# A recurrence's gate projections: the second and fourth weight sums of each strip formed by VectorE instead of GpSimd

## The chip, the cores and the metric

One core of one Trainium2 chip runs the whole program. The metric is device microseconds of one execution, the median of several runs. The engines named here are TensorE (PE in the profile, its weight loads apart as PEld), VectorE (DVE), ScalarE (ACT), GpSimd (POOL) and the DMA queue issued by SyncE (SPq).

## What is computed

Two transformer blocks of two layers each work on 256 latent and 256 context tokens, batch 1, in float32. The change lies in the first layer of the first block, an HGRN2 mixer with 16 heads of width 128:

```
q, i_in, f_fw, f_bw, z = jnp.split(h @ w_in, 5, axis=-1)     # h: 512 x 1024, w_in: 1024 x 10240
log_f = jnp.logaddexp(jnp.log(lbd), jnp.log1p(-lbd) + jax.nn.log_sigmoid(gf))
k = (1.0 - lbd) * jax.nn.sigmoid(-gf)
# per direction, a chunkwise scan  S_t = diag(f_t) S_{t-1} + k_t v_t^T,  o_t = S_t^T q_t
o = _rmsnorm(o, o_gain);  y = (o * silu(z)) @ w_out
```

Everything after it (latent attention, and the second block with its branches and convolutional feed-forward) is untouched.

## The kernel before

The engines' programs are written out by hand, each in its own order, and meet through semaphores. The mixer works on its 16 heads in 8 pairs. While the *core* of pair i-1 (the scan) runs, the *projections* of pair i run between its steps. This interleaving is a "round"; rounds 1 to 7 hold a core and projections, pair 0's projections stand ahead of them, and pair 7's core behind them is interleaved with the output projection.

A round's projections are five strips of w_in, 1024 x 256 each, loaded into five slots of `ring_mem`. Strips 0 to 3 (one forget gate, the readout gate z, the query, the other forget gate) are computed by a Strassen-Winograd scheme of seven products where eight would be plain: `hg_seven_tensor`, with `hg_parts` naming the quarters a11, a12, a21, a22 of a strip. Each product is 4 contraction steps of 128x128 weights against 256 tokens, all on line 805 (8 matmul instructions in the trace). The sums of tokens are made once, ahead of the rounds (`T_hg`, held in `xT`). The sums of weights are made for each strip:

- `S1_hg` = a21 + a22 (line 2301) and a21 := a11 - a21 (line 2302, raises `s3_ready`), by VectorE in `hg_sums_vector` at the end of the gathering of the strip before.
- a11 := S1_hg - a11 (line 2911, raises `s2_ready`) and a12 := a12 - a11 (line 2914, raises `s4_ready`), by GpSimd. These are the two that the change touches. They overwrite the strip in place, so the first must wait until product *one* has read a11, the second until product *two* has read a12: it waits for ScalarE's copies of those products out of PSUM (`one_kept`, line 1829; `two_kept`, line 1842).

TensorE's order in strip j of a round is, at step 2j: products one (a11), seven (a21), two (a12), seven's second half (a22); then a scan step's scores (line 911; two of them at step 0) and at some steps a conditioning product (line 544). At step 2j+1: product five (S1_hg); then **six** (a11, after `two_kept` and `s2_ready`); then five's second half (a12, after `five_kept` and `s4_ready`), which frees the strip; then the next scan step's scores.

VectorE's order is: for each scan step (`hg_scores_vector`) a key product (line 2256), a query product (line 2258, after TensorE's scores of the step), two predicated copies out of PSUM (line 2261), a product of totals (line 2263). After scan steps 1, 3, 5 and 7 comes the gathering of strip 0, 1, 2 and 3 (`hg_gather_vector`): part two plus one (line 2307), plus six (line 2309, after `six_full`, raises `u_ready`), then lines 2313, 2315 and 2318, then the next strip's first two sums. After scan step 4 VectorE multiplies the readout gate (line 2324), after step 6 the query (line 2328), each behind a ScalarE sigmoid (line 1860).

GpSimd has, besides those two sums of each strip, two copies at a round's end (`move_pool`, lines 2895 and 2899).

`nth(i, j)` is the count that a semaphore raised once a strip has reached by strip j of round i.

Of the kernel before, what the change touches and what calls it, by code (L numbers as in the profile page):

```python
# [42 lines left out]
def raised(n):  # L43


    return n + 1
# [112 lines left out]
def build(nc, w, const, out):  # L159

    F32, I32 = mybir.dt.float32, mybir.dt.int32
    ALU, ACT, AX = mybir.AluOpType, mybir.ActivationFunctionType, mybir.AxisListType.X
    V, S, PE = nc.vector, nc.scalar, nc.tensor
    ctx = ExitStack()
    with ctx:
# [3 lines left out]
        def sem(name):  # L169
            return ctx.enter_context(nc.semaphore(name))  # L170
# [4 lines left out]
        def view(ap, *dims, at=0):  # L175

            return bass.AP(ap.tensor, ap.offset + at, [list(ap.ap[0])] + [list(d) for d in dims])
# [59 lines left out]
        S1_hg = kT_flat[:, 0:512].rearrange("p (k n) -> p k n", k=4)  # L237
# [73 lines left out]
        if at.at > b_tables:  # L311
# [54 lines left out]
        one_kept, two_kept, five_kept, seven_kept = sem("one_kept"), sem("two_kept"), sem("five_kept"), sem("seven_kept")  # L366
        s3_ready, s2_ready, s4_ready, t_ready, u_ready, whole_ready = (
            sem("s3_ready"), sem("s2_ready"), sem("s4_ready"), sem("t_ready"), sem("u_ready"), sem("whole_ready"))
# [228 lines left out]
        def strip(name, j, k):  # L597
            return ring.slot(name, j).rearrange("p (k n) -> p k n", k=k)
# [186 lines left out]
        def nth(i, j):  # L785

            return i * 4 + (j - 3)

        def hg_parts(j):


            wj = strip("hg_in", j, 8)
            return wj[:, 0:4, 0:128], wj[:, 4:8, 0:128], wj[:, 0:4, 128:256], wj[:, 4:8, 128:256]
# [769 lines left out]
        def up_halves(l):  # L1563
            (_, a0, a1), (_, b0, b1) = halves(l)
            c0 = CTX * l
            return slice(c0 + a0, c0 + a1), slice(c0 + b0, c0 + b1), a1 - a0
# [253 lines left out]
        def hg_part(j, at, n):  # L1820
            return hg_whole[j][:, at:at + n]
# [474 lines left out]
        def hg_sums_vector(dve, st, i, j):  # L2296


            a11, _, a21, a22 = hg_parts(j)
            ring.wait_loaded(dve, "hg_in", j, i)  # L2300
            st.link(V.tensor_tensor(S1_hg, a21, a22, ALU.add))
            V.tensor_tensor(a21, a11, a21, ALU.subtract).then_inc(s3_ready, 1)

        def hg_gather_vector(dve, st, i, j):
            dve.wait_ge(one_kept, nth(i, j))
            dve.wait_ge(two_kept, nth(i, j))
            V.tensor_tensor(hg_part(j, 0, 256), hg_part(j, 0, 256), P1_hg, ALU.add)
            dve.wait_ge(six_full, nth(i, j))
            V.tensor_tensor(P1_hg, P1_hg, ps[:, 0, 256:512], ALU.add).then_inc(u_ready, 1)
            dve.wait_ge(u_ready, nth(i, j))  # L2310
            dve.wait_ge(seven_kept, nth(i, j))
            dve.wait_ge(five_kept, nth(i, j))
            st.link(V.tensor_tensor(hg_part(j, 256, 512).rearrange("p (s t) -> p s t", s=2), view(P1_hg, (0, 2), (1, 256)),
                                    P57_hg.rearrange("p (s t) -> p s t", s=2), ALU.add))
            st.mark(V.tensor_tensor(hg_part(j, 768, 256), hg_part(j, 512, 256), P57_hg[:, 0:256], ALU.add))
            dve.wait_ge(strips_used, ring.stages["hg_in"]["first"] + i * 5 + (j + 1))
            st.settle()
            V.tensor_tensor(hg_part(j, 256, 512), hg_part(j, 256, 512), ps[:, 1, :], ALU.add).then_inc(whole_ready, 1)
            if j < 3:
                hg_sums_vector(dve, st, i, j + 1)  # L2320
# [569 lines left out]
        def move_pool(pool, i):  # L2890

            if not (isinstance(i, int) and i == 0):
                pool.wait_ge(st_ready, i)
            wait_apart(pool, act_freed, i * 6 + 4)
            nc.gpsimd.tensor_copy(Tw, f_st.rearrange("p d c -> p (d c)"))
            if not (isinstance(i, int) and i == 0):
                pool.wait_ge(o_full, raised(i * 2))
            wait_apart(pool, act_freed, i * 6 + 6)
            nc.gpsimd.tensor_copy(v_w, v_st).then_inc(moved, 1)

        @block.gpsimd
        def _(pool):
            pool.dma_start(ident, const["ident"]).then_inc(tab_loaded, 16)
            pool.dma_start(masks_i, const["masks"]).then_inc(msk_loaded, 16)
            move_pool(pool, 0)
            with pool.Fori(1, PAIRS) as i:
                for j in range(4):
                    a11, a12, _, _ = hg_parts(j)
                    pool.wait_ge(s3_ready, nth(i, j))
                    pool.wait_ge(one_kept, nth(i, j))  # L2910
                    nc.gpsimd.tensor_tensor(a11, S1_hg, a11, ALU.subtract).then_inc(s2_ready, 1)
                    pool.wait_ge(two_kept, nth(i, j))
                    pool.wait_ge(s2_ready, nth(i, j))
                    nc.gpsimd.tensor_tensor(a12, a12, a11, ALU.subtract).then_inc(s4_ready, 1)
                move_pool(pool, i)
            pool.wait_ge(o_ready, raised(2 * PAIRS))
            pool.dma_start(ctx2_in, w["ctx_2"][0].rearrange("(g p) d -> p g d", p=128)).then_inc(ctx2_loaded, 16)
            nc.gpsimd.memset(poolw, 0.0).then_inc(pool_step, 1)
            for dst, name in ((cosb, "cosb"), (sinb, "sinb"), (rotb, "rotb"), (cosm, "cosm"), (sinm, "sinm"), (rotm, "rotm"),
                              (amask, "amask"), (poolm, "poolm"), (dftm, "dftm"), (dftc, "dftc")):  # L2920
                pool.dma_start(dst, const[name]).then_inc(tab_loaded, 16)
            pool.wait_ge(pool_step, 1)
            for l in range(2):
                for g in range(4):
                    e = g % 2 * 64
                    pool.dma_start(poolw[e:e + 64, l, g // 2, e:e + 64], w["pool_w_2"][l, g]).then_inc(tab_loaded, 16)

            steps = Steps(pool, pool_step)
            steps.n = 1
            G = nc.gpsimd  # L2930
            for l in range(2):
                a, b, hw = up_halves(l)
                h_rest, h_top = hT[:, 4:8, b], hT[:, 0:4, b]
                pool.wait_ge(h_ready, h_end[f"mix{l}_b"])
                G.tensor_tensor(T_mg[:, 0, :, 0:hw], h_rest, h_top, ALU.subtract).then_inc(mg_turned, 1)
                G.tensor_tensor(T_mg[:, 3, :, 0:hw], h_top, hT[:, 0:4, a], ALU.subtract).then_inc(mg_turned, 1)
                pool.wait_ge(mg_turned, 4 * l + 2)
                G.tensor_tensor(T_mg[:, 1, :, 0:hw], h_rest, T_mg[:, 3, :, 0:hw], ALU.subtract).then_inc(mg_turned, 1)
                pool.wait_ge(mg_turned, 4 * l + 3)
                G.tensor_tensor(T_mg[:, 2, :, 0:hw], hT[:, 4:8, a], T_mg[:, 1, :, 0:hw], ALU.subtract).then_inc(mg_turned, 1)  # L2940
                for s in range(MS):
                    a11, a12, _, _ = mg_parts(l, s)
                    sums = S_mg[s % 2]
                    pool.wait_ge(mg_first_sums, MS * l + s + 1)
                    steps.link(G.tensor_tensor(sums[:, 1], sums[:, 0], a11, ALU.subtract))
                    G.tensor_tensor(sums[:, 3], a12, sums[:, 1], ALU.subtract).then_inc(mg_sums, 1)

                pool.wait_ge(y_ready, raised(8 * l + 8))
                for f in range(FT):
                    t, j = f // 4, (f + 2) % 4  # L2950
                    ring.wait_loaded(pool, f"up{l}", j, t)
                    sums = S_up[:, f % 2]
                    a11, a12, a21, a22 = up_parts(l, f)
                    if f >= 2:
                        pool.wait_ge(first_sums_ready, (FT - 2) * l + f - 1)
                    else:
                        steps.mark(G.tensor_tensor(sums[:, 0], a21, a22, ALU.add))
                        G.tensor_tensor(sums[:, 2], a11, a21, ALU.subtract)
                        steps.settle()
                    steps.link(G.tensor_tensor(sums[:, 1], sums[:, 0], a11, ALU.subtract))  # L2960
                    G.tensor_tensor(sums[:, 3], a12, sums[:, 1], ALU.subtract).then_inc(sums_ready, 1)
# [95 lines left out]
```

## Time and profile before

| | |
|---|---|
| median of 3 runs | 2458.71 us (2458.56 to 2460.6) |
| the profiled execution | 2456.85 us, of which the profile's span is 2455.0 us |
| PE busy | 2382.2 us, 97% of the span |
| DVE busy | 1323.9 us, 54% |
| ACT busy | 597.3 us, 24% |
| POOL busy | 365.4 us, 15% |
| granted TensorE clock over the span | 0.994 of full speed |

The rounds lie between about 116 and 745 us. Shares over the whole span mix many stages. A round is read from the timeline, which lists each engine's instructions in order of their start, in microseconds from the span's start.

### The profile page before, as it was taken

What the parts mean: (1) busy time and instruction counts of PE and PEld (TensorE: products, weight loads), DVE (VectorE), ACT (ScalarE), POOL (GpSimd) and SP (SyncE); (2) the same over time, 40 slices, a digit from 0 to 9 for tenths busy, and PEclk for the clock granted to TensorE, in tenths of its full rate; (3) what the DMA queues carried; (4) which work ended last, traced back from release to release, by engine and by line L of the source; (5) the groups of instructions that cost most, each with busy time, mean ns of one, the idle gap of its engine ahead of it and who ended that gap; (6) DMA issues with size and microseconds to landing.
All of it is one profiled execution on the core that took longest, in us unless ns stands there. A gap on an engine that the chain in (4) does not pass through costs nothing.

```text
span 2455.0 us, 35576 instructions
## 1 busy us (share of the span) xinstructions
PE 2382.2 (97%) x14660; PEld 1930.0 (79%) x14660; DVE 1323.9 (54%) x2240; ACT 597.3 (24%) x1203; POOL 365.4 (15%) x250
## 2 busy tenths in 40 slices
PE   7999999999998999999999999999999999999999
PEld 3588888888875688668877778788884787999988
DVE  3186787787787233441263332366668335437951
ACT  3133333333222032342241000221110023113211
POOL 0012223222210100000101111022210000322310
PEclk9999999999998999999999999999999999999999
DMA  9433133223250525204311322233348551555662
GB/s 369 171 125 120 68 120 120 94 94 127 96 170 20 159 69 138 69 1 120 88 34 39 99 86 86 60 91 90 87 115 286 199 137 35 155 155 147 166 174 65
DMA packets 320819, 284.88 MB, mean 116 GB/s; under 512 B 27329, under 2 KB 300361, under 8 KB 320185
## 3 DMA queue, kind: packets, MB, share of 16 engines
q1 hardware_dynamic: 319002, 279.08, 37.2%
q0 software_dynamic: 1216, 3.93, 0.4%
q8 instruction: 89, 1.46, 0.2%
q14 instruction: 33, 0.27, 0.0%
q10 hardware_dynamic: 479, 0.13, 0.0%
HBM read 279.98 MB, written 3.15 MB: 115 GB/s over the span
## 4 chain that ended last, share of the span: by engine, by line
PE 87%; DVE 7%; ACT 2%; DMA 2%; issue 1%; SPq 1%; ACTq 0%; DVEq 0%
PE ps L805 13%; PE ps L1576 12%; PE ps L1489 8%; PE ps L1687 5%; PE ps L865 5%; PE ps L1672 4%; PE ps L1543 3%; PE ps L1522 3%; PE ps L911 2%; PE ps L856 2%; PE ps L998 2%; PE ps L1016 2%; PE ps L1090 2%; DVE arena L2668 2%; PE ps L1314 2%; PE ps L544 2%
## 5 line engine op out<-in xcount | busy, mean ns | idle before, releaser
L805 PE MATMUL ps<-hT,ring_mem 128*128 128x256 f32 x672 | 160.2, 381 | 0.0
L805 PE MATMUL ps<-xT,ring_mem 128*128 128x256 f32 x672 | 158.8, 379 | 0.0
L805 PEld LDWEIGHTS ps<-hT,ring_mem 128*128 128x128 f32 x672 | 126.0, 190 | 20.2 <-issue 3.2
L805 PEld LDWEIGHTS ps<-xT,ring_mem 128*128 128x128 f32 x672 | 127.6, 190 | 17.6 <-issue 0.3
L1576 PE MATMUL ps<-hT,arena 128*128 128x256 f32 (+1 forms) x704 | 132.5, 333 | 6.9 <-ACT hT L565 6.9
L468 DVE RECIPROCAL rstd<-root 128x256 f32<-128x256 f32 (+2 forms) x17 | 28.2, 1659 | 201.5 <-ACT root L441 200.4
L1576 PE MATMUL ps<-arena 128*128 128x256 f32 (+1 forms) x704 | 129.6, 327 | 0.0
L1576 PEld LDWEIGHTS ps<-hT,arena 128*128 128x128 f32 x704 | 112.2, 196 | 16.9 <-issue 7.5
L1576 PE MATMUL ps<-hT,ring_mem 128*128 128x256 f32 (+1 forms) x704 | 123.0, 327 | 0.0
L1672 PE MATMUL ps<-arena,ring_mem 128*128 128x512 f32 (+1 forms) x352 | 116.6, 492 | 2.2 <-DVE arena L2678 2.2
L1687 PE MATMUL ps<-arena,ring_mem 128*128 128x256 f32 (+1 forms) x704 | 118.2, 328 | 0.0
L1576 PEld LDWEIGHTS ps<-arena 128*128 128x128 f32 x704 | 109.7, 191 | 9.1
L1576 PEld LDWEIGHTS ps<-hT,ring_mem 128*128 128x128 f32 x704 | 107.9, 191 | 9.7 <-issue 0.6
L1687 PEld LDWEIGHTS ps<-arena,ring_mem 128*128 128x128 f32 x704 | 105.9, 191 | 11.4 <-issue 2.7
L865 PE MATMUL ps<-ring_mem,hT 128*128 128x256 f32 x512 | 113.0, 379 | 0.0
L865 PEld LDWEIGHTS ps<-ring_mem,hT 128*128 128x128 f32 x512 | 96.1, 190 | 12.4
L2960 POOL TENSOR_TENSOR arena<-arena,ring_mem 128x512 f32<-128x512 f32 x44 | 56.0, 1273 | 332.2 <-DVE arena L2686 332.2
L1672 PEld LDWEIGHTS ps<-arena,ring_mem 128*128 128x128 f32 x352 | 67.4, 193 | 48.1 <-issue 40.3
L2564 DVE TENSOR_TENSOR arena<-root,ps 128x256 f32<-128x256 f32 (+1 forms) x24 | 8.5, 354 | 175.4 <-ACT root L2094 124.1
L1489 PE MATMUL ps<-arena 128*128 128x256 f32 (+1 forms) x576 | 98.2, 327 | 0.0
L2608 DVE SCALAR_TENSOR_TENSOR xT<-ps,mod_b,xT 128x256 f32<-128x256 f32 (+1 forms) x60 | 23.5, 425 | 137.3 <-PE ps L1687 57.0
L1489 PEld LDWEIGHTS ps<-arena 128*128 128x128 f32 x576 | 87.8, 191 | 7.4
(348 smaller groups left out, 4669.9 us busy)
## 6 DMA issues: line engine op xcount, KB each, us to landing
ring_mem<-in_w_up_dram SPq DMA_DIRECT2D x88, 512.0 KB, 5.1
ring_mem<-in_hg_w_in_dram SPq DMA_DIRECT2D x40, 1024.0 KB, 5.0
ring_mem<-in_w_in_dram SPq DMA_DIRECT2D x30, 1024.0 KB, 5.5
ring_mem<-in_w_mod_dram SPq DMA_DIRECT2D x12, 2048.0 KB, 7.8
arena<-in_w_mod_dram SPq DMA_DIRECT2D x24, 1024.0 KB, 5.5
ring_mem<-in_w_down_dram SPq DMA_DIRECT2D x16, 1408.0 KB, 7.2
ring_mem<-in_ada_w_dram SPq DMA_DIRECT2D x8, 2048.0 KB, 7.7
ring_mem<-in_mla_w_in_dram SPq DMA_DIRECT2D x9, 1024.0 KB, 5.4
```

The source lines that it names most:

```text
L544: mm = PE.matmul(bank[c * 32:c * 32 + 32, 0:256], sil_cols[:, cond * 16 + 2 * k:cond * 16 + 2 * k + 32], wm[:, k % 4, c * 256:c * 256 + 25 ...
L805: mm = PE.matmul(dst, left[:, k, :], right[:, k, :], start=k == 0, stop=k == 3)
L856: mm = PE.matmul(bank, wj[:, k, m * 128:m * 128 + 128], hT[:, k, :], start=k == 0, stop=k == 7)
L865: mm = PE.matmul(bank[:, g * 256:g * 256 + 256], hT[:, k, tok:tok + 128], wj[:, k, :], start=k == 0, stop=k == 7)
L911: mm = PE.matmul(ps[c:c + w_, LV[b], (u % 4) * 128 + q0:(u % 4) * 128 + q0 + w_], keys, queries, start=True, stop=True)
L1489: mm = PE.matmul(mg_region(l, s, which, hw), left[:, k, :], right[:, k, 0:hw], start=k == 0, stop=k == 3)
L1522: mm = PE.matmul(ps[:, mg_bank(i) + m, 0:n], wj[:, k, m * 128:m * 128 + 128], brT[:, k, c0:T], start=k == k0, stop=k == k1 - 1)
L1543: mm = PE.matmul(ps[:, (0 if part == "_a" else 4) + j, m * (hi - lo):(m + 1) * (hi - lo)], wj[:, k, m * 128:m * 128 + 128], yT[:, k, c0 + ...
L1576: mm = PE.matmul(up_region(f, which, hw), left[:, k, :], right[:, k, 0:hw], start=k == 0, stop=k == 3)
L1672: mm = PE.matmul(ps[:, j, 0:n], wj[:, k, :], hid[:, k, 0:n], start=k == 0, stop=k == FT - 1)
L1687: mm = PE.matmul(ps[:, (4 if part == "_a" else 0) + j, 0:hi - lo], wj[:, k, :], hid[:, k, lo:hi], start=k == 0, stop=k == FT - 1)
L2960: steps.link(G.tensor_tensor(sums[:, 1], sums[:, 0], a11, ALU.subtract))
```

## The change

GpSimd's loop over the four strips is gone; it keeps its two copies. VectorE makes the two sums at the head of `hg_gather_vector`, ahead of its first addition, behind the same waits on `one_kept` and `two_kept`.

```diff
         def hg_gather_vector(dve, st, i, j):
+            a11, a12, _, _ = hg_parts(j)
             dve.wait_ge(one_kept, nth(i, j))
             dve.wait_ge(two_kept, nth(i, j))
+            V.tensor_tensor(a11, S1_hg, a11, ALU.subtract).then_inc(s2_ready, 1)
+            dve.wait_ge(s2_ready, nth(i, j))
+            V.tensor_tensor(a12, a12, a11, ALU.subtract).then_inc(s4_ready, 1)
             V.tensor_tensor(hg_part(j, 0, 256), hg_part(j, 0, 256), P1_hg, ALU.add)
             dve.wait_ge(six_full, nth(i, j))
...
             with pool.Fori(1, PAIRS) as i:
-                for j in range(4):
-                    a11, a12, _, _ = hg_parts(j)
-                    pool.wait_ge(s3_ready, nth(i, j))
-                    pool.wait_ge(one_kept, nth(i, j))
-                    nc.gpsimd.tensor_tensor(a11, S1_hg, a11, ALU.subtract).then_inc(s2_ready, 1)
-                    pool.wait_ge(two_kept, nth(i, j))
-                    pool.wait_ge(s2_ready, nth(i, j))
-                    nc.gpsimd.tensor_tensor(a12, a12, a11, ALU.subtract).then_inc(s4_ready, 1)
                 move_pool(pool, i)
```

The changed lines shift the numbers: line 2307 of before is 2311 in the changed kernel, 2309 is 2313, and the new sums are lines 2308 and 2310.

VectorE's instructions in the body of the loop over the rounds, around the gathering of strip 0. The first row of both is the last one of scan step 1. Before:

```order
L2263 TENSOR_TENSOR arena<-arena 128x1024 [waits merged]
L62 ISA
L2305 ISA [waits dve_step]
L2307 TENSOR_TENSOR arena<-arena 128x256 [waits two_kept,one_kept]
L2309 TENSOR_TENSOR arena<-arena,ps 128x256 [waits six_full]
L2313 TENSOR_TENSOR arena<-arena 128x512 [waits five_kept,seven_kept,u_ready]
```

And now:

```order
L2263 TENSOR_TENSOR arena<-arena 128x1024 [waits merged]
L62 ISA
L2306 ISA [waits dve_step]
L2308 TENSOR_TENSOR ring_mem<-arena,ring_mem 128x4x128 [waits two_kept,one_kept]
L2310 TENSOR_TENSOR ring_mem<-ring_mem 128x4x128 [waits s2_ready]
L2311 TENSOR_TENSOR arena<-arena 128x256
L2313 TENSOR_TENSOR arena<-arena,ps 128x256 [waits six_full]
L2317 TENSOR_TENSOR arena<-arena 128x512 [waits five_kept,seven_kept,u_ready]
```

Two instructions came in behind scan step 1's last product and ahead of the first addition, at each of the four strips; no register instruction came with them.

GpSimd's instructions in the body of its loop. Before, from the third strip on:

```order
L2911 TENSOR_TENSOR ring_mem<-arena,ring_mem 128x4x128 [waits one_kept,s3_ready]
L2914 TENSOR_TENSOR ring_mem<-ring_mem 128x4x128 [waits s2_ready,two_kept]
L2909 REGISTER_ALU
L2911 TENSOR_TENSOR ring_mem<-arena,ring_mem 128x4x128 [waits one_kept,s3_ready]
L2914 TENSOR_TENSOR ring_mem<-ring_mem 128x4x128 [waits s2_ready,two_kept]
L2911 TENSOR_TENSOR ring_mem<-arena,ring_mem 128x4x128 [waits one_kept,s3_ready]
L2914 TENSOR_TENSOR ring_mem<-ring_mem 128x4x128 [waits s2_ready,two_kept]
L36 ISA [waits st_ready]
L2895 COPY arena<-arena 128x2048 [waits act_freed]
```

And now, the whole body:

```order
L36 ISA [waits st_ready]
L2899 COPY arena<-arena 128x2048 [waits act_freed]
L2901 ISA
L36 REGISTER_ALU [waits o_full]
L2903 COPY arena<-arena 128x1024 [waits act_freed]
```

The eight sums of a round left GpSimd, the copies stayed. TensorE's and ScalarE's orders are the same in both kernels.

## Rows read from the trace of the kernel before

**Rows 1.** The page's chain of work that ended last, shares by engine.
```profile
PE 87%; DVE 7%; ACT 2%; DMA 2%; issue 1%; SPq 1%; ACTq 0%; DVEq 0%
```

**Rows 2.** Busy time by engine in one round: window, length, busy (count), PEclk, DMA.
```profile
383.00:472.00 89.00, 87.34 (x695) 74.12 (x694) 70.96 (x93) 29.13 (x45) 22.22 (x11) 1.00 0.31 105
```

**Rows 3.** Waits of PE in 110 to 790 us: us in total, times, longest.
```profile
PE ps L911 <- ACT K_c L1869: 18.0, 9, 6.1
```

**Rows 4.** Timeline, round 4, strip 0: start, duration, engine, line, operation.
```profile
394.47 2.23 DVE L2258 TENSOR_TENSOR arena<-arena 128x1024 f32<-128x1024 f32 x1
...
397.46 1.70 PEld L805 LDWEIGHTS ps<-xT,ring_mem 128*128 128x128 f32 x8
...
399.20 0.42 DVE L2307 TENSOR_TENSOR arena<-arena 128x256 f32<-128x256 f32 x1 [0.20 <-DVE arena L2263]
...
402.02 0.68 DVE L2301 TENSOR_TENSOR arena<-ring_mem 128x512 f32<-128x512 f32 x1
...
402.74 0.69 DVE L2302 TENSOR_TENSOR ring_mem<-ring_mem 128x512 f32<-128x512 f32 x1
```

**Rows 5.** Timeline, round 4, strip 1.
```profile
413.86 0.42 DVE L2307 TENSOR_TENSOR arena<-arena 128x256 f32<-128x256 f32 x1 [0.19 <-DVE arena L2263]
414.02 1.70 PEld L805 LDWEIGHTS ps<-xT,ring_mem 128*128 128x128 f32 x8
```

**Rows 6.** Timeline, round 4, strip 2.
```profile
425.51 1.72 POOL L2914 TENSOR_TENSOR ring_mem<-ring_mem 128x512 f32<-128x512 f32 x1 [2.11 <-ACT arena L1842]
426.01 2.30 DVE L2256 TENSOR_TENSOR arena<-arena 128x1024 f32<-128x1024 f32 x1
...
426.14 1.15 PE L911 MATMUL ps<-arena,K_c 128*64 128x64 f32 x32
...
428.23 1.21 DVE L2258 TENSOR_TENSOR arena<-arena 128x1024 f32<-128x1024 f32 x1
428.84 1.70 PEld L805 LDWEIGHTS ps<-xT,ring_mem 128*128 128x128 f32 x8
...
431.06 0.43 DVE L2307 TENSOR_TENSOR arena<-arena 128x256 f32<-128x256 f32 x1 [0.19 <-DVE arena L2263]
```

**Rows 7.** Timeline, round 4, strip 3.
```profile
440.78 1.15 PE L911 MATMUL ps<-arena,K_c 128*64 128x64 f32 x32
...
442.75 1.21 DVE L2258 TENSOR_TENSOR arena<-arena 128x1024 f32<-128x1024 f32 x1
443.48 1.70 PEld L805 LDWEIGHTS ps<-xT,ring_mem 128*128 128x128 f32 x8
...
445.32 0.42 DVE L2307 TENSOR_TENSOR arena<-arena 128x256 f32<-128x256 f32 x1
```

**Rows 8.** Timeline, round 7, strip 2 and the conditioning product behind it.
```profile
697.58 1.70 PEld L805 LDWEIGHTS ps<-xT,ring_mem 128*128 128x128 f32 x8
697.64 0.42 DVE L2307 TENSOR_TENSOR arena<-arena 128x256 f32<-128x256 f32 x1
...
703.67 1.93 PE L544 MATMUL ps<-ring_mem,sil_cols 128*32 128x256 f32 x32 [1.17 <-DMA ring_mem<-in_ada_w_dram]
```

**Rows 9.** Timeline, pair 7's core, scan step 1, no GpSimd work beside it.
```profile
755.05 2.22 DVE L2258 TENSOR_TENSOR arena<-arena 128x1024 f32<-128x1024 f32 x1
```

**Rows 10.** Timeline of PE alone, instructions behind three idle gaps elsewhere in the program.
```profile
789.07 1.98 PE L911 MATMUL ps<-arena,K_c 128*64 128x64 f32 x32 [2.65 <-ACT K_c L1869]
...
901.86 2.40 PE L1065 MATMUL ps<-hT,ring_mem 128*128 128x256 f32 x10 [2.61 <-issue]
...
2372.31 4.03 PE L1672 MATMUL ps<-arena,ring_mem 128*128 128x256 f32 x10 [2.16 <-DVE arena L2678]
```

**Rows 11.** Busy time by engine, with PEclk, in stretches behind those gaps.
```profile
788.50:795.20 6.70, 6.13 (x40) 3.85 (x41) 4.53 (x8) 0.51 (x1) 0.00 (x0) 0.50 0.01 2
899.30:906.00 6.70, 4.14 (x28) 3.31 (x32) 0.00 (x0) 5.17 (x16) 0.00 (x0) 1.00 0.54 159
...
2372.30:2375.50 3.20, 3.19 (x8) 2.45 (x9) 1.20 (x3) 0.31 (x1) 0.00 (x0) 0.50 0.02 6
```

## The prediction

> **What bounds the kernel now.** I read the chain of waits first: 87% of it is TensorE, 7% VectorE [rows 1]. GpSimd and VectorE therefore matter only where TensorE waits for them. Next the table of windows, one round at a time: in 89 us TensorE is busy 87.34 and VectorE 70.96, at the full clock [rows 2]. VectorE looks as if it had 18 us to spare in a round. Then the list of waits: through the whole recurrence TensorE's largest wait is 18 us, nine times, for the scan's keys from ScalarE [rows 3], and in none does it wait for GpSimd or for VectorE's gathering. So the two sums cost nothing today. What the changed kernel costs is decided in the timeline, by one comparison made at each strip: when does TensorE want a11, and when does VectorE come to its gathering? The weight load ahead of product six is the first; the start of line 2307 is the second, for the new sums stand exactly in its place. The reader is to see that in every strip VectorE is there about when six starts or later, though its average load is low: strip 0 at 399.20 against 397.46 [rows 4], strip 1 at 413.86 against 414.02 [rows 5], strip 2 at 431.06 against 428.84 [rows 6], strip 3 at 445.32 against 443.48 [rows 7].
>
> **What it removes.** GpSimd's 8 sums of a round. Nothing waited for them, so their time itself gives nothing. But one of them held up VectorE: in strip 2 the key product took 2.30 us, while a GpSimd sum that began 0.50 us before it ran [rows 6], and the query product of the same size took 1.21. Some 1.08 us of VectorE's time comes back there, and as much in strip 3, where the same pattern stands. How much of it counts is limited by TensorE's scores, for which the query product waits: in strip 2 they end at 427.29, so it can start near 427.34 instead of 428.23, a gain of 0.89; in strip 3 they end at 441.93, so 441.98 instead of 442.75, a gain of 0.77 [rows 6, 7]. In strip 0 the query product took 2.23 [rows 4], also beside a long GpSimd sum, but in pair 7's core the same product takes 2.22 with GpSimd idle [rows 9]: its access pattern costs that, and nothing comes back.
>
> **What it adds.** Two subtractions of 128x512 on VectorE at each of 28 strips. Line 2302 has the same form and takes 0.69 us; from line 2301 to its dependent 2302 it is 0.72 from start to start [rows 4]. So a11 is ready 0.69 after VectorE's arrival, and a12 1.41 after. Until TensorE's weight load starts I add 0.10; bounds are 0.04, the gap between 2301's end and 2302's start [rows 4], and 0.3. The stall of product six is then arrival + 0.79 - the load of before:
>
> - strip 0: 399.99 - 397.46 = 2.5 us
> - strip 1: 414.65 - 414.02 = 0.6 us
> - strip 2: 431.06 - 0.89 + 0.79 = 430.96, less 428.84 = 2.1 us
> - strip 3: 445.32 - 0.77 + 0.79 = 445.34, less 443.48 = 1.9 us
>
> Together 7.1 us a round. a12 is never late: its 0.72 us lie beside six, whose load takes 1.70. Nor does line 2307, now 1.41 later, make anything late: the next addition needs six, which is late itself. From line 2318 on VectorE waits for TensorE's last product of the strip and its lag starts afresh. At each strip the stall is therefore new and is not carried as a lag of VectorE's.
>
> Does the stall get lost later? The wait for keys at the head of a round [rows 3] is ScalarE's, which stands behind TensorE's own products of that round, so it moves along. At the round's end VectorE's states are needed by TensorE after a long values projection, and GpSimd's copies, unchanged, hang on those. Nothing there absorbs. SyncE's weight loads are issued on TensorE's release of a slot and move with it. Only round 7 differs. In its strip 2 the conditioning product of before ran late, so VectorE arrives with six (697.64 against 697.58); with the key product unblocked there too, the stall is about 0, and what is left falls into the 1.17 us that TensorE waits for a DMA right after [rows 8]. Round 7 costs 5.0. I take rounds 1 to 6 alike: 6 x 7.1 + 5.0 = 47.6 us.
>
> **The clock.** These are new idle gaps of TensorE, so I looked at what gaps of this size did elsewhere. After an idle gap of 2.65 us the granted clock was 0.50, the 1.2 GHz level, through 788.5 to 795.2; after one of 2.16 us it was 0.50 in 2372.3 to 2375.5; after one of 2.61 us it stayed 1.00, 2.4 GHz [rows 10, 11]. Of 13 new gaps above 2 us (7 in strip 0, 6 in strip 2) I let half end in a fall. A stretch like that of 2372.3, busy 3.19 of 3.20 us at half level, loses half of it, 1.6 us; where part of it lies in the gap, less: I take 1.5. That makes 6.5 x 1.5 = 10 us (bounds 0, and 20 gaps x 1.6 = 32 with strip 3's).
> By the Trainium skill (TensorE: Matmul & The Clock Gate, section HAM oscillation) only idle gaps longer than every one that this change makes let the clock fall in a kernel; by that this term is 0. The gap of 2.16 us in this trace speaks against it.
>
> **The sum.** 47.6 + 10 = 57.6 us on the profiled execution of 2456.85 gives 2514.4; the median of the runs, 2458.71, lies 1.86 above that execution, so I forecast **2516 us**. About 0.2% (5 us) is what a measurement of this kernel can tell from no change.
>
> **Rivals.**
>
> 1. *Stalls as worked out, no fall of the clock.* 2458.71 + 47.6 = 2506. For it: the clock is 1.00 throughout the rounds [rows 2] though they hold waits for keys. Against it: two of the three gaps in rows 10. The skill's rule named above leads here.
> 2. *Every gap of 1.9 us or more lets the clock fall.* 20 x 1.6 = 32 on top of 47.6: 2538. For it: two of three. Against it: the third, and strip 3's gap is shorter than any that is seen to do it.
> 3. *The stalls are partly absorbed.* If what TensorE waits for at a round's head did not move with it, 18 us over nine waits [rows 3], up to 2 each, 14 in seven rounds, could take up the stalls: 2458.71 + 34 to 44, about 2498. Against it: that wait's chain starts at TensorE.
> 4. *The other side: VectorE is in time, and it is not slower.* The mechanism is the hold of GpSimd on VectorE. If each of the 8 sums of a round cost VectorE the 1.08 us of the key product [rows 6], 8.6 us would come back in a round against 4 x 1.41 = 5.6 added, and VectorE would run ahead by 0.8 us a strip. It decides where line 2308 starts 0.8 us before six's load: from there no stall is left, and the time is 2459. Against it: the long query product without GpSimd [rows 9], that strip 0 alone would need 2.5 us, and that in strips 2 and 3 TensorE's scores set the limit.
>
> That the change does not do what it says is excluded by the order of instructions: GpSimd's sums are gone and VectorE's stand ahead of its first addition.
>
> **How the numbers follow.** My forecast, with about half of the gaps falling, 0.50; rival 1, 0.25; rival 2, 0.08; rival 3, 0.13; rival 4, 0.04, of which 0.01 would be faster by over 0.2%. The forecast's own case reaches from 2508 to 2524 (3 to 10 falls, and 0.04 to 0.3 us of hand-over at 27 stalls, which is -2 to +5). The range of 2499 to 2531 takes in rival 1 and most of rival 3, and the near side of rival 2; it leaves out rival 4 and the far ends. Faster 0.01, same 0.03, slower 0.96.
>
> **What would show it.** In the changed profile TensorE's list of waits gets a line, line 805 for VectorE's sum of a11 (line 2308), some 27 times, 45 to 50 us in total, the longest near 2.9. A round gets 96 us or more long against 89. In the timeline six's load follows the end of line 2308 by about 0.1, with a12's sum beside it; lines 2308 and 2310 take 0.69 each; the key products of strips 2 and 3 take 1.22. VectorE gains 56 x 0.69 = 39 us of busy time and gives back some 15; GpSimd loses about 100. PEclk shows some 0.5 stretches in the rounds. I am wrong if a round is under 93 us, if the waits for line 2308 fall under 30 us, or if the span grows by much more than those waits and the half-clock stretches explain. Should TensorE wait at `s4_ready` or `s3_ready` as well, VectorE is behind by more than a strip's slack, and the time is above my range.

## The result and the profile after

The changed kernel takes **2506.38 us** (four runs, 2506.3 to 2506.72), the kernel before 2458.64 in the same comparison: 1.0192 times as long, 95% interval 1.0178 to 1.0206. That is 47.7 us more.

TensorE's list of waits in 110 to 840 us, the same view as [rows 3]: us in total, times, longest.

```profile
PE ps L805 <- DVE ring_mem L2308: 38.5, 25, 2.6
PE ps L911 <- ACT K_c L1869: 17.0, 9, 6.1
```

The new first line is the whole story in short: product six waits for VectorE's sum of a11, 25 times. (Two more waits, of 0.12 us each, are too short for this list.) The wait for keys is as before.

The windows of one round, of three stretches at half clock and of one at full clock, as [rows 2] and [rows 11]: window, length, busy of PE, PEld, DVE, ACT and POOL, PEclk, DMA share, GB/s.

```profile
404.00:500.00 96.00, 88.54 (x696) 73.84 (x695) 74.49 (x100) 29.13 (x45) 5.16 (x2) 1.00 0.29 98
```

```profile
134.90:138.30 3.40, 3.40 (x10) 2.69 (x9) 1.54 (x3) 0.00 (x0) 0.00 (x0) 0.52 0.34 141
235.00:238.40 3.40, 3.40 (x35) 3.02 (x30) 3.37 (x5) 0.38 (x1) 0.00 (x0) 1.00 0.76 237
616.20:619.60 3.40, 3.40 (x9) 2.64 (x9) 1.53 (x3) 0.00 (x0) 0.00 (x0) 0.52 0.47 193
711.80:715.20 3.40, 3.40 (x9) 2.75 (x10) 0.90 (x2) 0.00 (x0) 0.00 (x0) 0.53 0.76 311
```

Against [rows 2] a round is some 7 us longer for the same 695 or so matmuls. TensorE's load is nearly the same, its idle time is not. The clock fell in three of the seven rounds (1, 6 and 7), each time behind strip 0's stall; the second row shows a stretch soon behind that stall in round 2, where it did not fall. Over the whole of round 2, 212 to 308 us, the granted clock is 1.00.

The timeline of round 4 in the changed kernel, strips 0 to 3, VectorE's new sums and product six. These lines answer to [rows 4 to 7].

```profile
418.60 1.59 PEld L805 LDWEIGHTS ps<-xT,arena 128*128 128x128 f32 x8 [0.41 <-issue]
...
421.95 0.69 DVE L2308 TENSOR_TENSOR ring_mem<-arena,ring_mem 128x512 f32<-128x512 f32 x1 [0.20 <-DVE arena L2263]
422.67 0.69 DVE L2310 TENSOR_TENSOR ring_mem<-ring_mem 128x512 f32<-128x512 f32 x1
422.75 1.59 PEld L805 LDWEIGHTS ps<-xT,ring_mem 128*128 128x128 f32 x8 [2.56 <-issue]
422.78 1.97 PE L805 MATMUL ps<-xT,ring_mem 128*128 128x256 f32 x8 [2.19 <-DVE ring_mem L2308]
...
437.61 1.59 PEld L805 LDWEIGHTS ps<-xT,arena 128*128 128x128 f32 x8 [0.41 <-issue]
...
439.85 1.59 PEld L805 LDWEIGHTS ps<-xT,ring_mem 128*128 128x128 f32 x8 [0.66 <-issue]
439.88 1.97 PE L805 MATMUL ps<-xT,ring_mem 128*128 128x256 f32 x8 [0.28 <-DVE ring_mem L2308]
...
451.73 1.22 DVE L2256 TENSOR_TENSOR arena<-arena 128x1024 f32<-128x1024 f32 x1
...
452.94 1.59 PEld L805 LDWEIGHTS ps<-xT,arena 128*128 128x128 f32 x8
453.06 1.22 DVE L2258 TENSOR_TENSOR arena<-arena 128x1024 f32<-128x1024 f32 x1
...
456.69 1.59 PEld L805 LDWEIGHTS ps<-xT,ring_mem 128*128 128x128 f32 x8 [2.15 <-issue]
456.72 1.96 PE L805 MATMUL ps<-xT,ring_mem 128*128 128x256 f32 x8 [1.78 <-DVE ring_mem L2308]
...
469.61 1.59 PEld L805 LDWEIGHTS ps<-xT,arena 128*128 128x128 f32 x8
...
473.12 1.59 PEld L805 LDWEIGHTS ps<-xT,ring_mem 128*128 128x128 f32 x8 [1.91 <-issue]
473.15 1.96 PE L805 MATMUL ps<-xT,ring_mem 128*128 128x256 f32 x8 [1.54 <-DVE ring_mem L2308]
```

In each strip the first PEld row is product five's load and the second is six's. Before, six's load began 1.62 us after five's in all 28 strips; in strip 0 of round 4 it stood at 397.46 [rows 4], and five's was this row of the kernel before:

```profile
395.84 1.59 PEld L805 LDWEIGHTS ps<-xT,arena 128*128 128x128 f32 x8 [0.41 <-issue]
```

Now it is 4.15, 2.24, 3.75 and 3.51 us, so six is late by 2.53, 0.62, 2.13 and 1.89 us. Product six's load starts 0.12 us after line 2308 ends, in all 28 strips, and line 2310 runs beside it. In strip 2 the key product (line 2256) takes 1.22, no longer 2.30.

The page's line of busy times: VectorE 1345.4 us (1323.9 before), GpSimd 253.7 (365.4).

```profile
PE 2395.1 (96%) x14660; PEld 1931.9 (77%) x14660; DVE 1345.4 (54%) x2296; ACT 597.2 (24%) x1203; POOL 253.7 (10%) x194
```

**Where the time went, by the starts in the two timelines.** The profiled spans are 2455.0 and 2504.5, 49.5 apart. From round 1's product one to the output products that close round 7 it is 623.3 us before and 673.3 after, so the rounds hold 50.0; ahead of them the changed execution is 0.7 longer and behind them 1.2 shorter. Rounds 2 to 5 each grew by 6.77 us (89.23 to 96.0). Round 6, with a fall of the clock, took 97.67, so a fall costs 1.67. Three falls at that price are 5.0 us, and the stalls are the other 45: 6 x 6.77 and 4.3 in round 7.

### The profile page after: what moved, and what is told of

The parts are those of the page before. It is cut to its first block, busy times and chain, and to the rows that moved or that the text cites. A ratio compares the mean times of both kernels' runs of the same rounds, so it can differ in the third digit from the quotient of the medians.

```text
span 2504.5 us, 35494 instructions
## 1 busy us (share of the span) xinstructions
PE 2395.1 (96%) x14660; PEld 1931.9 (77%) x14660; DVE 1345.4 (54%) x2296; ACT 597.2 (24%) x1203; POOL 253.7 (10%) x194
## 4 chain that ended last, share of the span: by engine, by line
PE 83%; DVE 10%; ACT 2%; issue 2%; DMA 2%; SPq 1%; DVEq 0%; ACTq 0%
PE ps L1576 11%; PE ps L805 11%; PE ps L1489 8%; PE ps L1687 4%; PE ps L865 4%; PE ps L1672 4%; PE ps L1543 3%; PE ps L1522 3%; PE ps L856 2%; PE ps L998 2%; PE ps L1016 2%; PE ps L1090 2%; PE ps L911 2%; DVE arena L2672 2%; DVE arena L2258 2%
## 5 line engine op out<-in xcount | busy, mean ns | idle before, releaser
L805 PE MATMUL ps<-xT,ring_mem 128*128 128x256 f32 x672 | 163.5, 387 | 38.8 <-DVE ring_mem L2308 38.5
```

Source lines behind the costliest of these rows:

```text
L805: mm = PE.matmul(dst, left[:, k, :], right[:, k, :], start=k == 0, stop=k == 3)
```

## The experiments

Each ran against the kernel before on the same chip. "The rounds" is the length from round 1's product one to the products that close round 7 in the profiled execution: 623.3 us before, 673.3 in the changed kernel. The edits of "No sums at all", "One strip alone" and "More work ahead" are shown against the changed kernel, the others against the kernel before.

### No sums at all

```diff
-            V.tensor_tensor(a11, S1_hg, a11, ALU.subtract).then_inc(s2_ready, 1)
-            dve.wait_ge(s2_ready, nth(i, j))
-            V.tensor_tensor(a12, a12, a11, ALU.subtract).then_inc(s4_ready, 1)
...
-            pe.wait_ge(s2_ready, nth(i, j))
...
-            pe.wait_ge(s4_ready, nth(i, j))
```

> Leaves out both later weight sums of every strip: no engine forms them, and TensorE multiplies the unsummed quarters. Theory (the sums cost only by the place at which VectorE forms them; on GpSimd they cost nothing): as before, 2457 to 2460 us, the wait of line 805 for a sum gone, a round about 89.2 us. Rival (GpSimd's sums held up VectorE, and so TensorE): under 2452 us. If GpSimd's sums are no help at all, key products of strips 2 and 3 take 1.2 us and nothing else moves.

Measured: 2458.2 us, 0.9997 times before (0.9988 to 1.0007). The rounds take 622.8 us, 89.23 each as before. VectorE's busy time is 1308.7 us, 15.2 less than before though its work is the same: this is what GpSimd's sums cost VectorE. TensorE saw nothing of it. So the two sums cost the kernel before nothing, and the holds of 1.08 us fell into VectorE's slack. The rival falls.

### Only a12's sum on VectorE

```diff
         def hg_gather_vector(dve, st, i, j):
             dve.wait_ge(one_kept, nth(i, j))
             dve.wait_ge(two_kept, nth(i, j))
+            dve.wait_ge(s2_ready, nth(i, j))
+            V.tensor_tensor(a12, a12, a11, ALU.subtract).then_inc(s4_ready, 1)
...
                     nc.gpsimd.tensor_tensor(a11, S1_hg, a11, ALU.subtract).then_inc(s2_ready, 1)
-                    pool.wait_ge(two_kept, nth(i, j))
-                    pool.wait_ge(s2_ready, nth(i, j))
-                    nc.gpsimd.tensor_tensor(a12, a12, a11, ALU.subtract).then_inc(s4_ready, 1)
```

> GpSimd forms a11, VectorE forms a12 alone at the head of its gathering. Theory (a stall is VectorE's arrival plus 0.79 us less the time at which TensorE wants that quarter): a12 is wanted 1.73 us later than a11, so stalls of 0.8, 0, 0.4 and 0.1 us in strips 0 to 3, 1.3 a round, 8 to 9 in all: 2466 us, 2463 to 2470. Rival (VectorE's load: half of the added work gives half of the added time): 2482 us.

Measured: 2466.38 us, 1.0033 times (1.0023 to 1.0042), 7 to 8 us more. TensorE's new wait is here, in the list of 110 to 840 us:

```profile
PE ps L805 <- DVE ring_mem L2309: 4.1, 7, 0.8
```

From six's first matmul to the next product's it is 2.39 us in strip 0 and 1.98 in strip 2 where it was 1.73, so stalls of 0.66, 0, 0.25 and 0 us, a little under the expected 0.8, 0, 0.4 and 0.1. A whole round grew by 1.1 to 1.2 us where 1.3 was expected; what makes up the 0.2 to 0.3 beyond the two stalls was not traced. The rounds take 631.0 us. Half of the added VectorE work costs a sixth of the added time, since a12 is wanted 1.73 us later.

### Only a11's sum on VectorE

```diff
             dve.wait_ge(one_kept, nth(i, j))
             dve.wait_ge(two_kept, nth(i, j))
+            V.tensor_tensor(a11, S1_hg, a11, ALU.subtract).then_inc(s2_ready, 1)
...
-                    pool.wait_ge(s3_ready, nth(i, j))
-                    pool.wait_ge(one_kept, nth(i, j))
-                    nc.gpsimd.tensor_tensor(a11, S1_hg, a11, ALU.subtract).then_inc(s2_ready, 1)
                     pool.wait_ge(two_kept, nth(i, j))
```

> VectorE forms a11 alone at the head of its gathering, GpSimd forms a12 behind it. Theory: the whole stall of the changed kernel is a11's, so it stays: 2503 to 2510 us, the upper end where GpSimd's sum, 1.3 to 1.7 us from a11's end, comes after TensorE is through with product six. Rival (VectorE's load): 2482 us.

Measured: 2507.78 us, 1.02 times (1.0183 to 1.0217). The rounds take 673.0 us, the changed kernel's to 0.3, and the clock falls in the same three places. The other half of the added work costs all of the time. Together with the last one this shows that what counts is not how much VectorE does.

### Both sums on VectorE, at earlier places

```diff
+                if gates:
+                    hg_second_sum_vector(dve, i + 1, 0)
                 hg_scores_vector(dve, st, i, 0)
                 for term in range(1, 8):
-                    hg_scores_vector(dve, st, i, term)
+                    if gates and term % 2 and term > 1:
+                        hg_second_sum_vector(dve, i + 1, term // 2)
+                    hg_scores_vector(dve, st, i, term, gates)
...
             V.tensor_tensor(comb(Qw, h), comb(Qw, h), view(Tw, (2 * h, n), (PC - h, 2), (0, h), at=h), ALU.mult).then_inc(merged, 1)
+            if gates and term % 2:
+                hg_fourth_sum_vector(dve, i + 1, term // 2)
```

The two helpers hold a11's and a12's sum with the waits that they had.

> VectorE forms both sums as in the changed kernel, but a11 ahead of the scan step before the gathering (in strip 0 ahead of the scan step 0) and a12 behind that step's query product. Theory (place, not load): both are there when TensorE wants them, but for up to 0.4 us of a12 or of later work in strips 2 and 3: 2457 to 2464 us. Rival (VectorE's load, or GpSimd's missing share): about 2506 us as in the changed kernel.

Measured: 2458.69 us, 1.0002 times (0.9992 to 1.0012): the time of before, with all of the change's work on VectorE and none on GpSimd. Strip 2 of a round in its timeline:

```profile
425.47 0.68 DVE L2245 TENSOR_TENSOR ring_mem<-arena,ring_mem 128x512 f32<-128x512 f32 x1
...
426.68 1.59 PEld L805 LDWEIGHTS ps<-xT,arena 128*128 128x128 f32 x8
...
428.30 1.70 PEld L805 LDWEIGHTS ps<-xT,ring_mem 128*128 128x128 f32 x8
428.35 0.68 DVE L2251 TENSOR_TENSOR ring_mem<-ring_mem 128x512 f32<-128x512 f32 x1
```

a11's sum (line 2245 here) is done 2.15 us before six's load, which stands 1.62 behind five's as it should; a12's (line 2251) lies beside six. VectorE is busy 1339.5 us, and a round takes 89.25. The rival of VectorE's load is refuted, and the whole 48 us is a matter of two instructions' place in one engine's order.

### One strip alone on VectorE

```diff
-            V.tensor_tensor(a11, S1_hg, a11, ALU.subtract).then_inc(s2_ready, 1)
-            dve.wait_ge(s2_ready, nth(i, j))
-            V.tensor_tensor(a12, a12, a11, ALU.subtract).then_inc(s4_ready, 1)
+            if j in (0,):
+                V.tensor_tensor(a11, S1_hg, a11, ALU.subtract).then_inc(s2_ready, 1)
+                dve.wait_ge(s2_ready, nth(i, j))
+                V.tensor_tensor(a12, a12, a11, ALU.subtract).then_inc(s4_ready, 1)
...
+                for j in (1, 2, 3):
```

followed in GpSimd's program by its two sums as before. The second kernel has strip 1 in place of strip 0.

> Only strip 0's two sums on VectorE, those of strips 1 to 3 on GpSimd as before. Theory (each strip's stall stands by itself): product six of strip 0 stalls 2.5 us and then runs about 0.1 faster, so 2.4 in seven rounds, 17 us: 2475 us without a fall of the clock, 2480 if three gaps end in one as in the changed kernel. Rival (the strips' stalls hang together, VectorE's lag being handed on): clearly more than 17 plus 5. Rival (VectorE's load): a quarter of 48 us, 2471.

> Only strip 1's two sums on VectorE. Theory: 0.5 us in each of seven rounds, 3.5 us: 2462 us, 2461 to 2464, and no fall of the clock, since no gap is over 1 us. Rival (VectorE's load): a quarter of 48 us, 2471.

Measured, strip 0: 2481.3 us, 1.0093 times (1.0076 to 1.011). The rounds take 646.0 us, 22.7 more; three falls of the clock are 5.0 of that, and 17.7 are seven stalls of 2.5. Strip 1: 2462.77 us, 1.0016 times (1.0006 to 1.0025), no fall, rounds 626.6 us, 3.3 more. Strips add up: 17.7 and 3.3 leave 24 of the 45 us for strips 2 and 3, and the timeline's 2.1 in six rounds and 1.9 in seven, less 0.1 each, make 24.6.

### More work ahead of a11's sum

```diff
+            V.tensor_tensor(hg_part(j, 256, 512).rearrange("p (k n) -> p k n", k=4), S1_hg, S1_hg, ALU.subtract)
+            V.tensor_tensor(hg_part(j, 768, 256).rearrange("p (k n) -> p k n", k=2), S1_hg[:, 0:2], S1_hg[:, 0:2], ALU.subtract)
             V.tensor_tensor(a11, S1_hg, a11, ALU.subtract).then_inc(s2_ready, 1)
```

The first kernel has the first of the two lines, the second has both.

> The changed kernel with one more subtraction of 128x512 on VectorE ahead of a11's (its result is overwritten unread). From start to start such instructions stand 0.61 us apart. Theory (TensorE loses whatever VectorE comes later, one for one): 27 stalls longer by 0.61 us, 16.5 us: 2523 us with as many falls of the clock as in the changed kernel; each further fall adds 1.7 us, and with half of the 20 gaps of 2.5 us and over falling, 2535. Rival (slack elsewhere takes it): under 2515.

> The changed kernel with one subtraction of 128x512 and one of 128x256 more on VectorE ahead of a11's (results overwritten unread): 0.95 us later. Theory: 27 x 0.95 = 26 us on 2506: 2532 us with three falls of the clock in the rounds. Gaps are then near 3.5, 1.6, 3.1 and 2.8 us. If the length of the gap decides over the clock, most of the 20 gaps over 2.5 us fall, adding up to 29 us, 2561; if not, three or four fall again.

Measured, one more: 2537.37 us, 1.0317 times (1.03 to 1.0334); one and a half: 2554.11 us, 1.038 times (1.0363 to 1.0398). The rounds take 701.2 and 718.0 us. The clock was at half level behind ten stalls in the first and behind thirteen in the second, where two of the stretches lasted twice as long, so that I count 15 (the longer stretch cost its round 1.4 us more than a short one). Taking 10 x 1.67 and 15 x 1.67 off leaves 61.2 and 69.7 us over before, where 45 + 16.5 = 61.5 and 45 + 26 = 71 were expected. TensorE loses what VectorE comes later, nearly one for one.

The two kernels also say which gaps let the clock fall. By TensorE's idle time ahead of six, in rounds 1 to 6:

| | strip 0 | strip 2 | strip 3 |
|---|---|---|---|
| changed kernel | 2.2 us (2.6 in round 1): 2 of 6 | 1.8: none | 1.5: none |
| one more | 2.8 (3.2): all 6 | 2.4 (2.2 in round 1): 4 of 6 | 2.14: none |
| one and a half more | 3.1 (3.5): all 6 | 2.7 (2.6): all 6 | 2.48: none of 6 |

In round 7 strip 0 stood idle for 2.5 us in the changed kernel and for 3.4 in the last one, with a fall in both, and for 3.1 us with one more, without any. Longer idle time mostly means more falls at the same strip. But strip 3 stood idle for 2.48 us six times without one, and strip 2 for 2.38 with a fall in four of five. Nor is it the place alone: with strip 0's sums alone on VectorE its stall was as long as in the changed kernel, 2.2 us in rounds 2 to 6, and there round 4 had the fall and round 6 had none. From the last kernel, two such stalls on TensorE alone and the stretch behind each:

```profile
275.76 3.65 PE L805 MATMUL ps<-xT,ring_mem 128*128 128x256 f32 x8 [2.71 <-DVE ring_mem L2310]
...
294.81 1.53 PE L805 MATMUL ps<-xT,ring_mem 128*128 128x256 f32 x6 [2.48 <-DVE ring_mem L2310]
```

```profile
275.80:279.20 3.40, 3.40 (x8) 2.77 (x9) 0.88 (x2) 0.00 (x0) 0.00 (x0) 0.50 0.00 0
294.80:301.60 6.80, 6.54 (x37) 5.67 (x38) 5.44 (x7) 2.37 (x5) 0.00 (x0) 1.00 0.24 74
```

Product six takes 3.65 us at the 1.2 GHz level; at the 2.4 GHz level it took 1.97 in the changed kernel's rows. What decides beside the idle time and the strip was not tried.

### The wait at a round's head

The sums cost nothing once well placed, on either engine, so a gain had to come from a wait that TensorE has in both kernels: the 1.41 us at a round's head for ScalarE's copy of step 1's keys. This is its row in round 4 of the kernel before:

```profile
392.50 1.55 PE L911 MATMUL ps<-arena,K_c 128*64 128x64 f32 x32 [1.41 <-ACT K_c L1869]
```

VectorE stands idle there for 5 us, and GpSimd, free of its sums, for longer. Three kernels move that copy. The first two differ only in the sums: at the early places on VectorE, or on GpSimd as before.

```diff
             if term == 1:
-                act.wait_ge(unpacked, i + 1)
-            else:
-                act.wait_ge(merged, i * LEVELS + term - 1)
+                return
+            act.wait_ge(merged, i * LEVELS + term - 1)
...
             V.tensor_tensor(k_sum, k_st[:, 0, :], k_st[:, 1, :], ALU.add).then_inc(unpacked, 1)
+            dve.wait_ge(unpacked, i + 1)
+            V.tensor_copy(view(K_c, (2, PC // 2), (1, 2), (1, 1)), comb(Kw, 1)).then_inc(kc_ready, 1)
```

The third has its sums at the early places on VectorE, as the first, and the same copy in GpSimd's program, at the head of its loop.

> Both sums on VectorE at their early places, and the copy of the keys for scan step 1 made by VectorE right behind its unpacking instead of by ScalarE. At a round's head VectorE stood idle for 5 us while TensorE waited 1.41 us for ScalarE's copy, which stood behind square roots and a table load. Theory (TensorE's order is the bound, so a wait that it loses counts in full): the scores of step 1 then wait only for VectorE's copies of step 0, about 1.1 us earlier, seven rounds, 8 us: 2451 us, 2448 to 2454. Rival (the added VectorE work of 1 to 2 us in a round costs somewhere): 2459 or more.

> The kernel before (sums on GpSimd) with only the keys of step 1 copied by VectorE. Theory: the same 8 us, 2451, since neither place of the sums is waited for. If the freed GpSimd or its hold on VectorE matters once the round's head is shorter, the one with sums on VectorE at early places is faster by 2 us or more.

> As e11_keys_vector, but the keys of step 1 are copied by GpSimd, which has no sums left to make. From the end of VectorE's unpacking to TensorE's scores of step 0 there are 5 us, and a GpSimd copy of 2048 elements took 2.1: it should be there in time, so 2451 us as with VectorE. If its two strides make it longer than some 5.5 us it comes late, and the gain shrinks towards 2459.

Measured: 2451.5 us with the sums and the keys on VectorE, 0.9974 times before (0.9962 to 0.9985); 2454.69 us with the sums on GpSimd, 0.9983 (0.9974 to 0.9992); 2453.11 us with the keys on GpSimd, 0.9977 (0.9968 to 0.9986). All three beat both kernels, by 7, 4 and 5.5 us against the kernel before where 8 was expected of each. The intervals overlap, so which is best in time stays open. The rounds take 618.4, 619.1 and 618.7 us, 4 to 5 less than before; each of rounds 2 to 6 went from 89.23 to 88.28, 88.48 and 88.29. That is 0.95 us where the sums are on VectorE, a little under the 1.1 expected, and 0.75 where they are on GpSimd. The round's head in the first of them:

```profile
384.46 0.84 DVE L2241 COPY K_c<-arena 128x1024 f32<-128x1024 f32 x1
...
388.77 1.15 PE L911 MATMUL ps<-arena 128*64 128x64 f32 x32
389.51 1.29 DVE L2260 COPY arena<-ps 128x512 f32<-128x512 f32 x2 [3.61 <-PE ps L911]
...
390.25 1.55 PE L911 MATMUL ps<-arena,K_c 128*64 128x64 f32 x32 [0.33 <-DVE arena L2260]
```

The keys are there 3.5 us ahead of the scores of step 0, and what TensorE still waits for is VectorE's copy of those scores, 0.33 us. Most of the missing 0.1 us is a new wait: VectorE's own sum of strip 1, a21, now comes just late for product seven of that strip, whose load waits 0.25 us for it.

The expected 8 us counted the wait in seven rounds. In the kernel before only rounds 2 to 6 have it at 1.41 us; in rounds 1 and 7 the same scores waited 0.33 and 0.42 us for VectorE's copy of the scores before them, and those rounds gained next to nothing. Five rounds of 0.95 are 4.8 us, as the rounds show. That the median of the first kernel lies 7 us below is not explained by its rounds.

The kernel with its sums on GpSimd also answers the question of its own expectation. There the sum of a12 begins half a microsecond ahead of VectorE's key product of step 1, which takes 2.82 us instead of 2.22; VectorE comes later to everything behind it, and product seven of strip 1 waits longer:

```profile
391.77 1.27 POOL L2915 TENSOR_TENSOR ring_mem<-ring_mem 128x512 f32<-128x512 f32 x1 [4.58 <-ACT arena L1842]
392.32 2.82 DVE L2257 TENSOR_TENSOR arena<-arena 128x1024 f32<-128x1024 f32 x1
...
403.74 1.59 PEld L805 LDWEIGHTS ps<-xT,ring_mem 128*128 128x128 f32 x8 [0.45 <-DVE ring_mem L2303]
```

So once the round's head is shorter, GpSimd's sums do cost something: 0.2 us in each of rounds 2 to 6. That is about 1 us, and the medians' distance of 3 us is more than it explains.

## Why the prediction was right, and where not

The forecast was 2516 us in a range of 2499 to 2531, and 2506.4 was measured. The time is that of rival 1 to a tenth.

- *What bounds the kernel: TensorE, and the sums on GpSimd cost nothing.* Right; without any sums it is 2458.2.
- *The place decides, and the stall of a strip is VectorE's arrival + 0.79 us less the time of before.* Right in every strip: 2.5, 0.6, 2.1 and 1.9 worked out, 2.53, 0.62, 2.13 and 1.89 in the trace. The hand-over was 0.12 where 0.10 was taken.
- *What comes back from GpSimd's hold in strips 2 and 3 is bounded by TensorE's scores.* Right in both: the key product takes 1.22, and strip 2's query product starts at 453.06, 0.05 after TensorE's scores end. That the long query product of strip 0 is its own and not GpSimd's is right as well: it takes 2.25 in the changed kernel.
- *7.1 us a round.* A little high: 6.77. After a stall product six's loads take 1.59 us instead of 1.70, 0.1 at each strip. Round 7 was 4.3, not 5.0.
- *a12 is never late, and nothing absorbs the stalls.* Right, by a11's sum alone (2507.8) and by the slope of one with more work ahead of it. But rival 3 misread [rows 3]: of those nine waits only five, of 1.41 us, stand at the heads of rounds; the other four, 11 us of the 18, are in pair 7's core behind the rounds. So the heads could have absorbed 7 us at the most, not 14.
- *The clock: half of 13 gaps above 2 us, 1.5 us each, 10 us.* This is the term that failed. Its count was of lateness from load to load and not of idle time: the queue of matmuls still runs when the next load would begin, so 2.5 and 2.1 us of lateness are 2.2 and 1.8 us of idle time in the changed timeline. Only strip 0's seven gaps were above 2 us, and behind three of them the clock fell. The cost of one was sized well, 1.67. So the term was 5 us, not 10. On the profiled executions the sum was 47.6 + 10 = 57.6 and the measured one is 45 + 5 in the rounds less 0.5 around them, 49.5. That the time agrees with rival 1 is luck and no proof of it: it has no fall of the clock, and there were three. Its stalls were 2.6 us too large, the falls add 5.0, 0.5 comes off around the rounds, and the medians lie 1.8 us closer together than the profiled executions.
- *The Trainium skill's rule.* By it (the Trainium skill, TensorE: Matmul & The Clock Gate, section HAM oscillation) no gap of this change is long enough. The trace does not agree: the clock fell behind idle times of 2.2 to 2.6 us here, in three rounds, and with more work ahead behind all 12 of 2.8 us and more in strip 0 of rounds 1 to 6.
- *What would show it*: the wait for line 2308 was there, with 38.5 us in 25 waits where I gave 45 to 50 in 27, because idle time is shorter than lateness and two of the waits are too short for the list. The longest was 2.6, not 2.9. VectorE's busy time grew by 21.5 us, which is the 39 of the new sums less 17 given back, where some 15 was said; GpSimd lost 112 rather than 100.

## What to carry to other kernels

Before moving work to an engine that is only half busy, read from the timeline when that engine comes to the place where the work is put, and when the consumer wants it: the price is that difference, strip by strip, and the average load says nothing of it. If the engine comes late, look for an earlier place in its order where the inputs are already there; here that took the whole 48 us away. Before counting a wait once for every round, look at it in each round. Count idle time of TensorE from matmul to matmul when the clock is at issue, and lateness from load to load when time is.

## What the runs showed of the hardware

- A GpSimd subtraction of 128x512 that began beside VectorE's two long products took 5 us in rounds 2 to 6 of the kernel before, where in strip 2 the same one took 1.72 [rows 6]. Its row in round 4 is below. The other way round, a VectorE product of 1.22 us took 2.30 when a GpSimd sum had begun 0.5 us ahead of it. Without them VectorE gets back 15.2 us over 56 GpSimd instructions, 0.3 each on average.

```profile
392.72 4.99 POOL L2914 TENSOR_TENSOR ring_mem<-ring_mem 128x512 f32<-128x512 f32 x1 [5.97 <-ACT arena L1842]
```

- TensorE's clock fell at idle times from 2.2 us on at some places and stayed up at 2.48 at another, and once at 3.1, so the length alone does not tell. In round 6 of the changed kernel a fall cost 1.67 us.
- The four runs of the changed kernel lie within 0.4 us, those of the kernel before, in the comparisons of this study, between 2455.9 and 2463.1. The same three rounds fell in the changed kernel and in the one with a11's sum alone.
